# A top-k search's 31 steps dealt out differently over the items of a projection stage

## What is computed

```python
def second_block(x, ...):
    proj = rms_norm_2(h, g) @ w_in
    rq, rk, rv, rg, aq, ak, av, iq, ik, iw = split_columns(proj)
    ret_out = retention(rope(rq), rope(rk), rv, rg)          # chunk by chunk, gated by silu(rg)
    att_out = dsa_attention(rope(aq), rope(ak), av, ...)     # each query attends to its 256 best keys
    ...

def dsa_attention(...):
    iscore = einsum('bths,bth->bts', relu(einsum('bthe,bse->bths', qi, ki)), wi)
    iscore = where(causal, iscore, -inf)
    _, sel = lax.top_k(iscore, 256)
    # softmax attention over the selected keys alone
```

## Time and profile before

| | us |
|---|---|
| three runs | 2909.23, 2909.64, 2915.69; median 2909.64 |
| the profiled execution | 2909.0 |
| its span, first to last instruction | 2907.1 |
| PE busy in the span | 2763.0 (95%) |
| DVE, ACT, POOL busy | 1793.3 (62%), 1236.0 (43%), 1201.9 (41%) |

### The profile page before, as it was taken

How to read it: one execution, slowest core, us unless ns; L and a number is a source line. 1 busy time by engine, 2 the same in 40 slices (tenths; PEclk the granted TensorE clock), 3 DMA queues, 4 the chain that set the end, 5 groups by cost and what they waited for, 6 DMA issues and landing times. The chain is left out here.

```text
span 2907.1 us, 38766 instructions
## 1 busy us (share of the span) xinstructions
PE 2763.0 (95%) x13644; PEld 2260.1 (78%) x13644; DVE 1793.3 (62%) x2683; ACT 1236.0 (43%) x2258; POOL 1201.9 (41%) x848
## 2 busy tenths in 40 slices
PE   5999999999999999999998889978899999999998
PEld 4877788887788888888887667856678888887887
DVE  6748757323676666522846888774557777776153
ACT  5225545101533333323644667545443444443243
POOL 4011222434634444534641243531173456665454
PEclk7999999999999999999999899999999999999999
DMA  6531111323421222254520123100151221224452
GB/s 247 162 116 30 30 44 56 111 65 102 138 91 55 87 87 87 81 180 157 191 87 8 37 69 106 44 8 1 41 185 51 80 87 67 77 87 159 156 188 91
DMA packets 176236, 272.35 MB, mean 94 GB/s; under 512 B 13144, under 2 KB 105560, under 8 KB 176088
## 3 DMA queue, kind: packets, MB, share of 16 engines
q1 hardware_dynamic: 176088, 270.39, 28.2%
HBM read 224.21 MB, written 46.14 MB: 93 GB/s over the span
## 5 line engine op out<-in xcount | busy, mean ns | idle before, releaser
L2071 POOL TENSOR_TENSOR sb_out_lo<-sb_out_raw,sb_out_hi 128x512 fp32r<-128x512 f32 (+1 forms) x174 | 313.0, 1807 | 311.5 <-ACT sb_out_hi L2058 311.4
L133 PE MATMUL psum<-sb_out_hi,sb_a_hi 128*128 128x512 f32 x912 | 358.5, 393 | 5.5 <-ACT sb_junk L2282 4.4
L135 PE MATMUL psum<-sb_out_hi,sb_a_lo 128*128 128x512 f32 x912 | 355.8, 390 | 0.0
L134 PE MATMUL psum<-sb_out_lo,sb_a_hi 128*128 128x512 f32 x912 | 355.7, 390 | 0.0
L1544 POOL TENSOR_TENSOR sb_pair_lo<-sb_pair_sum,sb_pair_hi 128x512 fp32r<-128x512 f32 x180 | 237.1, 1329 | 269.5 <-ACT sb_pair_hi L1688 269.5
L133 PE MATMUL psum<-sb_h_hi,sb_w_hi 128*128 128x512 f32 x640 | 256.5, 401 | 2.9 <-DVE sb_h_lo L2218 2.4
L135 PE MATMUL psum<-sb_h_hi,sb_w_lo 128*128 128x512 f32 x640 | 249.7, 390 | 0.0
L134 PE MATMUL psum<-sb_h_lo,sb_w_hi 128*128 128x512 f32 x640 | 249.6, 390 | 0.0
L133 PE MATMUL psum<-sb_h_hi,sb_pair_hi 128*128 128x512 f32 x576 | 224.1, 389 | 0.0
L134 PE MATMUL psum<-sb_h_lo,sb_pair_hi 128*128 128x512 f32 x576 | 224.1, 389 | 0.0
L135 PE MATMUL psum<-sb_h_hi,sb_pair_lo 128*128 128x512 f32 x576 | 224.1, 389 | 0.0
(11 more groups left out here) (487 smaller groups left out, 6378.4 us busy)
## 6 DMA issues: line engine op xcount, KB each, us to landing
act_kept<-sb_gate_up SPq DMA_DIRECT2D x40, 512.0 KB, 3.0
sb_pairs_raw<-in_w_up SPq DMA_DIRECT2D x18, 1024.0 KB, 5.2
sb_late_w<-in_w_ada SPq DMA_DIRECT2D x32, 512.0 KB, 4.6
sb_w_raw<-in_w_in SPq DMA_DIRECT2D x54, 256.0 KB, 3.1
sb_out_raw<-in_w_ffn_down SPq DMA_DIRECT2D x44, 256.0 KB, 3.0
sb_out_raw<-in_w_down SPq DMA_DIRECT2D x44, 256.0 KB, 2.8
sb_act_ring<-act_kept SPq DMA_DIRECT2D x40, 256.0 KB, 3.9
sb_act_late<-act_kept SPq DMA_DIRECT2D x40, 256.0 KB, 4.1
```

Source lines behind the costliest of these rows:

```text
L133: nc.tensor.matmul(out, stationary.hi, moving.hi, start=start, stop=False)
L134: nc.tensor.matmul(out, stationary.hi, moving.lo, start=False, stop=False)
L135: return nc.tensor.matmul(out, stationary.lo, moving.hi, start=False, stop=stop)
L2071: self.nc.gpsimd.tensor_tensor(w.lo, raw, w.hi.bitcast(F32), ALU.subtract).then_inc(self.w_lo, 1)
```

## The change

One table is replaced. `STEPS` is now the running sum of `STEPS_IN`, which says how many steps stand in each item.

```diff
-STEPS = [max(n - 1, 0) for n in range(4 * TB)] + [BITS] * 11
+STEPS_IN = [0, 1, 1, 1, 1, 1, 1, 0] + [1, 1, 1, 1, 1, 1, 1, 0] * 2 + [1, 1, 2, 1, 2, 1, 2, 1]
+STEPS = [sum(STEPS_IN[:n]) for n in range(4 * TB)] + [BITS] * 11
```

## The result

The change makes the kernel slower: a median of 2933.48 us (2928.68 to 2935.15, four runs) against 2911.22 (2909.23 to 2915.69, four runs), a ratio of 1.0071 with a 95% interval of 1.0057 to 1.0085. The direction is the forecast one; the time lies outside the range of 2912 to 2928. The profiled execution took 2932.23 us, its span is 2930.4, 23.3 longer than before.

What follows compares the result with a forecast made beforehand. PE was taken to set the pace in the gate chunk, so whatever makes it wait there adds time. Profiled 2909.0 - 2.8 (junction) + 14.7 (three double items) = 2920.9 us, 0.4% slower; range 2912 to 2928.

Steps and rivals of the forecast that it cites:

- The empty items: Q7, K7 and V7, left without a step: two give nothing, K7 gives a gain of 2.8 us.
- Q7 and V7: Emptying them gives nothing: at Q7 the step saved is spent waiting, at V7 PE does not wait before.
- K7: Hole before V0/V1 shrinks from 8.42 to 1.8 us; a second wait of 3 to 5 us appears mid-pair.
- the junction: From K7 to V0/V1 and V2: V2 starts at 1746.85 instead of 1749.64, gain 2.8 us, bounds 1.7 to 4.9.
- the Trainium skill's rule on the shared ports: DVE and POOL lock each other out; with compares on fewer low parts the junction would gain 3.1 instead of 2.8 us.
- The double items: G2, G4 and G6, two steps each: each costs 3.1 + 1.8 = 4.9 us, three 14.7, bounds 8.7 to 19.8.
- The wait: In G3, G5 and G7 PE waits 3.1 us for ACT's copy of turned keys, delayed by second counts; bounds 2.9 to 3.7.
- The clock: Behind each double item's wait PE's lowered clock costs 1.8 us more, between 0 and 2.9.
- the three holes that I took it from: PE waits of 8.42 us before V0/V1, 2.34 before Q6's turned rows, 1.60 before tile 2's turned keys; clock loss 2.9, 1.7, 1.7.
- The counts were not hidden: Rival, chance 0.10: ACT's 4.7 us of idling per gate item hides the second counts, doubles cost nothing, 2906.2 us.
- the hole did not go whole: Rival, chance 0.06: V's slices 4 to 7 come early enough, junction gains 9.5 us, doubles hidden, 2899.5 us.
- The clock holds: Rival, chance 0.20: holes of 2 to 5 us leave PE at 2.4 GHz; doubles cost 9.3, junction gains 4.6, 2913.7 us.

Runs made afterwards that it cites:

- The run with late counts: Changed kernel, with ACT's second counts behind the gate and copy of turned keys, and DVE's scores prepared ahead of the second step: 2922.03 us.
- two runs that differ in POOL's order alone: Changed kernel with late counts, Q7 and K7 empty, doubles in G2 and G5: 2914.26 us; with POOL adding item 6's rows behind one low part, not four: 2905.04.

## Why the prediction was wrong, point by point

**The empty items.** Q7 and V7: right. DVE's first decide in K1 comes 77.90 us after the stage's first matmul, before 77.87. K7: both waits came as written, 1.73 us (1.8 forecast) and 4.51 (3 to 5); PE resumes in the pair 12.47 us after K7's last matmul, against 12.48 worked out. Only the clock behind it was mis-sized: the 24 matmuls take 8.40 us at 0.64 instead of 5.57, so 2.8 us are lost, not 1.8. Hence 1.8 us gained at the junction, not 2.8 (1.7 was the lower bound). The 0.3 us that the Trainium skill's rule on the shared ports ("SBUF — State Buffer", "SBUF: two separate sides") would have added didn't come: POOL's four low parts took 5.28 us instead of 5.38, and its addition behind them 1.47 instead of 1.27. DVE's three compares, from 1733.52 for 3.89 us, still fell beside the last low parts and the start of that addition.

**A gain that was not in the sum.** Behind the 1.60 us before the turned keys of tile 2 the clock held at 1.00 in the changed kernel; before it was 0.60. That gave 1.6 us back.

**The double items.** The wait: right, 2.90 us three times, the lower bound of 2.9 to 3.7, with the releaser and the places named. The clock: **this is the step that failed.** I took 1.8 us per wait, between 0 and 2.9, from the three holes of the earlier trace rows. It was 4.67, 4.40 and 4.06, beyond the bound. The size of this term was wrong, not its place. All three holes that I took it from are followed by dense matmuls of 128x512 directly or after four short ones; the three new ones are followed by some 40 small matmuls of the outputs. The run with dense matmuls put behind the wait gives 1.3 to 1.6 us, near the forecast's 1.8: that was about right for a place that the change doesn't have. The prediction asked whether the small matmuls "didn't feel" the clock and allowed 0 for it; it did not ask the other question, whether they bring it back. A fourth hole of the stage, which the earlier trace rows leave out, would not have warned of it. It stands before the turned rows of Q0, again with dense matmuls behind four short ones, and lost 2.2 us over 4.40, within the bounds (its row, and the window behind it with the columns of the earlier trace rows):

```profile
1641.65 1.11 PE L3411 MATMUL psum<-sb_consts,sb_rotated 128*128 128x128 f32 x4 [4.47 <-POOL sb_rotated L3624]
```

```profile
1641.60:1646.00 4.40, 4.35 (x13) 3.57 (x14) 4.30 (x15) 3.01 (x6) 0.00 (x0) 0.50 0.00 0
```

**The sum.** Forecast +11.9; the stage gave +19.5: 22.6 for the doubles instead of 14.7, 1.6 to 1.8 gained at the junction instead of 2.8, and 1.6 gained at the turned keys. Of the 22.6, 8.7 are waiting and 13.1 clock; the rest is small. On the forecast's base of 2909.0 the 19.5 give 2928.5, just above the range; the profiled run's 2932.23 holds 4.27 us more, by which the stage began later, and this is chance, which no term of the sum could have had. (The upper bound of the wait, 3.1 and half a microsecond, is 3.6 and not 3.7; that moves the range by 0.3 us.) The sign was right because the waiting alone was larger than any gain of the junction.

**The rivals.** The counts were not hidden, and the hole did not go whole, for the reasons given. "The clock holds" is refuted for waits of 2.90 us (six of six fell, with the run that has dense matmuls behind) and true for those of 1.50 (three of three held). The run with late counts adds a rival that I had not listed: the second step delays DVE, and through POOL's queue the next chunk's weights. In the changed kernel that was hidden because PE was late by its own waits.

## What to carry to other kernels

A wait's price is its length plus what the lowered clock costs behind it, and the second term depends on what runs there: 1.3 to 1.6 us behind 2.9 us of idling with dense 128x512 matmuls, 4.1 to 4.7 with a series of small ones. Take that term only from a hole that has the same kind of work behind it.
Before extra work is put on an engine that looks idle, read its queue in order: here ACT had 4.7 us free in each item, but behind the copy that PE waits for. Moving the counts behind that copy brought a double item's cost in the gate chunk from 7.5 us down to 1.7 (12.95 us from turned keys to turned keys, 11.22 in an item with one step), as long as the last double did not delay the next chunk's weights. The one gain of 9 us lay in a queue that the change didn't touch, POOL's: two runs that differ in POOL's order alone took 2914.26 and 2905.04. It stands on the empty K7; in the kernel before, POOL's addition of K6 waits for DVE until 1735.76, and there the order was not tried.

## What the runs showed that I had not expected

Useless matmuls made the changed kernel 12.6 us faster: 36 of them, in a place where PE would have idled.

Between a wait that leaves the clock alone and one that lowers it there is no single length in these traces. Behind 1.50 us it held three times, behind 2.2 it fell one time in three, behind 2.9 six times in six. But behind 1.60 and 1.74 us before the turned keys of tile 2 it fell in both traces of the kernel before, and held behind 1.60 to 1.76 us at the same place in all nine traces of the other kernels. Before V0 it held behind 1.73 to 1.89 us in the same nine, and before the turned rows of Q6 it fell behind 2.34 and 2.75 us in all ten traces that have that wait. The junction of V0 and V1 differs ahead of the keys of tile 2, and so does the order of DVE's and ACT's work; which of them decides, if either does, was not tried and stays open.
